# Seven block products of 256 x 512 x 512 in place of eight for most of the second feed-forward products, with weight sums made by accumulating transfers

## The reference

```python
x = x + jnp.concatenate([ya, yb, yc], axis=-1) @ w_out
u = _rms(x, norm2) @ w_ff1                  # 1024 -> 4096
return x + jnp.square(jax.nn.relu(u)) @ w_ff2   # 4096 -> 1024
```

## Time and profile before

| | |
|---|---|
| median of 3 runs | 2929.8 us (2923.84 to 2934.4) |
| profiled execution, span from the first to the last instruction | 2923.6 us |
| mean granted clock of TensorE | 0.969 of 2.4 GHz |
| PE / DVE / ACT / POOL busy | 95% / 49% / 34% / 6% |
| bytes moved by DMA | 216.83 MB, 74 GB/s over the span |

### The profile page before, as it was taken

How to read it: one execution, slowest core, us unless ns; L and a number is a source line. 1 busy time by engine, 2 the same in 40 slices (tenths; PEclk the granted TensorE clock), 3 DMA queues, 4 the chain that set the end, 5 groups by cost and what they waited for, 6 DMA issues and landing times.

```text
span 2923.6 us, 45193 instructions
## 1 busy us (share of the span) xinstructions
PE 2783.6 (95%) x20028; PEld 2299.7 (79%) x20028; DVE 1440.3 (49%) x2242; ACT 988.4 (34%) x1490; POOL 170.2 (6%) x166
## 2 busy tenths in 40 slices
PE   8989999999989999999999799999999897999998
PEld 7877888878768888887768778888887587788887
DVE  4575533344475444433454574343634645743436
ACT  4344322233344232323342233232333522332422
POOL 0200000001100000000013300000000033000000
PEclk9998999999989999999989899999999898999999
DMA  5102222223003222221000033222220001132221
GB/s 192 50 1 97 87 101 96 92 73 114 17 8 136 94 94 101 93 92 52 15 1 30 20 128 115 90 102 90 85 73 29 1 3 46 73 130 101 87 101 58
DMA packets 31011, 216.83 MB, mean 74 GB/s; under 512 B 3680, under 2 KB 3936, under 8 KB 6368
## 3 DMA queue, kind: packets, MB, share of 16 engines
q1 hardware_dynamic: 30816, 213.94, 20.2%
HBM read 211.83 MB, written 2.10 MB: 73 GB/s over the span
## 4 chain that ended last, share of the span: by engine, by line
PE 88%; DVE 8%; ACT 2%; issue 1%; PEld 0%; PEldq 0%; DMA 0%; ACTq 0%; SPq 0%; DVEq 0%
PE PS L570 81%; PE PS L573 3%; PE PS L771 2%; DVE SC L1381 2%; DVE X L1389 1%; DVE R L1381 1%; DVE SM L1392 1%; PE PS L1185 1%; PE PS L1135 1%; DVE LN L1381 0%; PE PS L855 0%; DVE SM L1381 0%; ACT LN L2172 0%; PE PS L764 0%; PEld PS L570 0%
## 5 line engine op out<-in xcount | busy, mean ns | idle before, releaser
L570 PE MATMUL PS<-H,SPL 128*128 128x512 f32 (+1 forms) x4560 | 1054.2, 391 | 5.5 <-DVE H L1389 4.0
L570 PEld LDWEIGHTS PS<-H,SPL 128*128 128x128 f32 (+1 forms) x4560 | 851.5, 188 | 188.5 <-issue 7.0
L1381 DVE TENSOR_TENSOR SPL<-RAW,SPL 128x2048 fp32r<-128x2048 f32 (+3 forms) x192 | 429.6, 2239 | 680.5 <-ACT SPL L2172 677.5
L2172 ACT ACTIVATE SPL<-RAW 128x2048 fp32r<-128x2048 f32 (+3 forms) x192 | 358.0, 1868 | 783.0 <-PE PS L570 754.8
L570 PE MATMUL PS<-SPL,Uu 128*128 128x512 f32 x2592 | 589.8, 389 | 0.0
L570 PEld LDWEIGHTS PS<-SPL,Uu 128*128 128x128 f32 x2592 | 486.5, 188 | 101.0
L570 PE MATMUL PS<-SPL,H 128*128 128x512 f32 (+2 forms) x2016 | 432.1, 375 | 2.3 <-DVE SPL L1381 1.6
L570 PEld LDWEIGHTS PS<-SPL,H 128*128 128x128 f32 x2016 | 363.7, 189 | 69.2 <-DVE SPL L1381 2.1
L2172 ACT ACTIVATE R<-PS 128x512 f32<-128x512 f32 (+1 forms) x154 | 88.5, 584 | 187.0 <-PE PS L570 156.3
L1381 DVE TENSOR_TENSOR R<-R,PS 128x512 f32<-128x512 f32 (+1 forms) x98 | 64.8, 661 | 106.6 <-PE PS L570 91.2
L2172 ACT ACTIVATE Uu<-R 128x512 fp32r<-128x512 f32 x108 | 68.3, 632 | 142.2 <-DVE R L1381 142.2
(11 more groups left out here) (240 smaller groups left out, 2481.7 us busy)
## 6 DMA issues: line engine op xcount, KB each, us to landing
RAW<-in_wA SPq DMA_DIRECT2D x84, 1024.0 KB, 4.8
RAW<-in_wB SPq DMA_DIRECT2D x84, 1024.0 KB, 4.8
RAW<-in_wAo SPq DMA_DIRECT2D x8, 1024.0 KB, 4.8
RAW<-in_wBo SPq DMA_DIRECT2D x8, 1024.0 KB, 5.0
LN<-in_ln SPq DMA_DIRECT2D x4, 1024.0 KB, 6.6
P<-in_pB SPq DMA_DIRECT2D x2, 1920.0 KB, 9.1
RAW<-in_wBm SPq DMA_DIRECT2D x4, 704.0 KB, 4.0
X<-in_x SPq DMA_DIRECT2D x4, 512.0 KB, 5.6
```

The lines of the kernel that those rows point to most:

```text
L570: return pe.matmul(out, l_, r_, start=start, stop=stop)
L1381: return v.tensor_tensor(out, a, b, o)
L2172: return a.activation(out, in_, f, scale=scale)
```

## The change

In a changed pass (all four in layers 0 and 1, the first two in each layer of the second half) the second product is computed as a 2 x 2 block product with seven multiplications. The left operand A has tokens 0 to 255 (EARLY) or 256 to 511 (LATE) by features 0 to 511 or 512 to 1023 of the pass; the right operand B has the same halves of features by the two halves of the output columns, so a block of B is one weight group. Each of the seven products (P1, P2, P5, P3, P6, P7, P4, in this order) is 24 matmuls in two banks. P3 is accumulated on P5's banks after P5 was added to X, P6 on P1's, P7 on P6's. DVE makes the four sums of A (S1 to S4, in place). The four sums of B (T1 to T4) are made by transfers that POOL issues with an add: T3 = B12 + B22 and T1 = B11 + B12 and T2 = T1 + B22 from device memory onto a loaded group, T4 = B21 + T2 from one on-chip buffer onto another. T1 is issued when B11 has been split, T2 when T1 has, T4 when T2 has landed and B21 has been split. The raw groups have four buffers (the two of `RAW`, `RW2`, and `LN`, which held norm tables); each of the seven factors is split into high and low as a group was, so a pass has seven splits in place of four for the second product. DVE makes 16 additions into X per pass, in place of 8.

In layers 0 and 1 the norm's factor now goes in ahead of the square: PE spreads the four tiles' roots over a bank (`spread_roots`, between the first two groups of the stretch), ACT copies it to `RB`, DVE computes max(u, 0) x RB out of the bank (`squared`), and ACT squares in place. A's high and low parts are made 1024 columns at a time (`high_operand`, `low_operand`). The program's scratch for descriptors that POOL writes is 1024 bytes per partition, in place of the default.

```diff
+N_UP = ((4, 4, 4, 4), (4, 4, 4, 4), (8, 8, 6), (8, 8, 6))
+PRODUCTS = ("P1", "P2", "P5", "P3", "P6", "P7", "P4")
+FACTORS = ("B11", "B21", "T1", "B22", "T2", "T3", "T4")
+HELD = {"B11": "B11", "B21": "B21", "T1": "B11", "B22": "B22", "T2": "B11", "T3": "B12", "T4": "B21"}
+SUMS = {"T3": 1, "T1": 1, "T2": 2, "T4": 3}
+CHAINED = 3
+BLOCKS = {"B11": 0, "B21": 1, "B12": 2, "B22": 3}
...
+            if p in QUADS[l]:
+                held = dict(zip(("B11", "B21", "B22", "B12"), ring))
+                landed = {name: load(l, at + BLOCKS[name], slot)[1] for name, slot in held.items()}
+                summed = {name: (name != "T3", 16 * ((1 if name == "T3" else CHAINED) * len(quads) + k)) for name, k in SUMS.items()}
+                quads.append((l, p, len(splits), at, held, landed, summed))
+                for name in FACTORS:
+                    split(held[HELD[name]], landed.get(name), summed.get(name))
+                last[held["B11"]] = len(splits)
+                ring = [held[n] for n in ("B22", "B12", "B21", "B11")]
...
+        A11, A21, A12, A22 = (RU[k][:, :, ts_] for k in range(2) for ts_ in (EARLY, LATE))
+        S3, S2, S1, S4 = A11, A11, A21, A12
+        RB = SM[:, 0:512]
...
+        LEFT = {"P1": ("A11", 1), "P2": ("A12", 3), "P5": ("S1", 4), "P3": ("S4", 6), "P6": ("S2", 5), "P7": ("S3", 2),
+                "P4": ("A22", 7)}
+        PBANKS = {"P1": (0, 1), "P2": (2, 3), "P5": (4, 5), "P3": (4, 5), "P6": (0, 1), "P7": (0, 1), "P4": (6, 7)}
...
+            def spread_roots(l):
+
+                pe.wait_ge(s.nr, 8 * (l + 1))
+                bank_free(4)
+                for t in range(4):
+                    ins = mm(bank(4)[:, t * 128:(t + 1) * 128], rms[t][:, 1:2].to_broadcast([128, 128]), C("ident"))
+                ins.then_inc(s.gtr, 1)
+                free[4] = (s.rc, l + 1)
+
+            def quad(key):
+
+                base, ready = n["xadd"], n.get("ul", 0)
+                added_to = {("P6", 0): 1, ("P6", 1): 2, ("P3", 0): 5, ("P3", 1): 6, ("P7", 0): 9, ("P7", 1): 10}
+                for name in PRODUCTS:
+                    i = at["group"]
+                    at["group"] += 1
+                    wh_, wl_ = slot(i)
+                    which, lows = LEFT[name]
+                    ah, al = operand(OPERANDS[which][0])
+                    pe.wait_ge(s.lo, i + 1)
+                    pe.wait_ge(s.ul, ready + lows)
+                    goes_on = (name, 0) in added_to
+                    for b in range(2):
+                        if goes_on:
+                            pe.wait_ge(s.xadd, base + added_to[name, b])
+                        else:
+                            bank_free(PBANKS[name][b])
+                        out = bank(PBANKS[name][b])
+                        for k in range(4):
+                            sl = slice(k * 256 + b * 128, k * 256 + b * 128 + 128)
+                            wh, wl = wh_[:, k * 512:(k + 1) * 512], wl_[:, k * 512:(k + 1) * 512]
+                            pe.matmul(out, ah[:, sl], wh, start=k == 0 and not goes_on, stop=False,
+                                      skip_group_check=True)
+                            pe.matmul(out, ah[:, sl], wl, start=False, stop=False, skip_group_check=True)
+                            ins = pe.matmul(out, al[:, sl], wh, start=False, stop=k == 3, skip_group_check=True)
+                        assert done_mm(ins) == full_at[(*key, name), b]
+                    assert at["mm"] == used_at[i]
+                for b, e in enumerate((12, 14, 3, 4, 7, 8, 15, 16)):
+                    free[b] = s.xadd, base + e
+                n("xadd", 16)
...
+            def low_operand(which, ks=slice(0, 4)):
+
+                i, a_ = OPERANDS[which]
+                hi, lo = operand(i)
+                v.wait_ge(s.uh, n("uh"))
+                ins = tt(four(lo)[:, ks], a_[:, ks], four(hi)[:, ks].bitcast(f32), ALU.subtract)
+                if ks.stop == 4:
+                    ins.then_inc(s.ul, 1)
+                    n("ul")
+
+            def row_sum(which):
+
+                if which == "S3":
+                    ins = tt(S3, A11, A21, ALU.subtract)
+                elif which == "S1":
+                    ins = tt(S1, A21, A22, ALU.subtract)
+                elif which == "S2":
+                    ins = stt(S2, A22, -1.0, S3, ALU.mult, ALU.subtract)
+                else:
+                    ins = tt(S4, A12, S2, ALU.add)
+                ins.then_inc(s.us, 1)
+                v.wait_ge(s.us, n("us"))
...
+                def add(name, b, t, h, first=False, op=ALU.add):
+                    ps = bank(PBANKS[name][b])
+                    v.wait_ge(s.mm, full_at[(*key, name), b])
+                    if (h, t) in last_sum:
+                        v.wait_ge(s.xadd, last_sum[h, t])
+                    if first and beta is not None:
+                        stt(Xh(h, t), Xh(h, t), beta, ps, ALU.mult, op).then_inc(s.xadd, 1)
+                    else:
+                        tt(Xh(h, t), Xh(h, t), ps, op).then_inc(s.xadd, 1)
+                    last_sum[h, t] = n("xadd")
...
+                low_operand("A12", slice(2, 4))
+                row_sum("S1")
+                low_parts()
+                low_operand("S1")
+                add("P1", 0, 0, 0, True)
+                add("P1", 1, 1, 0, True)
+
+                row_sum("S2")
+                add("P2", 0, 0, 0)
+                low_operand("S2")
+                row_sum("S4")
+                low_parts()
+                add("P2", 1, 1, 0)
+
+                low_operand("S4")
+                add("P5", 0, 2, 1, True)
+                low_parts()
+                add("P5", 1, 3, 1, True)
+
+                add("P3", 0, 0, 1, True)
+                low_parts()
+                add("P3", 1, 1, 1, True)
+
+                low_operand("A22")
+                low_parts()
+                add("P6", 0, 0, 1, op=ALU.subtract)
+                ended(0)
+                add("P6", 1, 1, 1, op=ALU.subtract)
+                ended(1)
+
+                low_parts()
+                add("P7", 0, 2, 0, True)
+                add("P7", 0, 2, 1, op=ALU.subtract)
+                add("P7", 1, 3, 0, True)
+                add("P7", 1, 3, 1, op=ALU.subtract)
+
+                low_parts()
+                add("P4", 0, 2, 0)
...
+                    def squared(q, b):
+                        v.wait_ge(s.mm, full_at[(l, "up", p, q), b])
+                        stt(RU[q][:, b], bank(sets[q][b]), 0.0, RB, ALU.max, ALU.mult).then_inc(s.fv, 1)
+
+                    paid()
+                    low_parts()
+                    low_parts()
+                    v.wait_ge(s.rc, l + 1)
+                    for b in range(4):
+                        squared(0, b)
...
+            def quad(l, p):
+
+                j, at, held, landed, summed = quads[l, p]
+
+                def block(name):
+                    return stream[first_load(l) + at + BLOCKS[name]][0]
+
+                B11, B21, B12 = (raw_slots[held[name]][:, 0:2048] for name in ("B11", "B21", "B12"))
+
+                g.wait_ge(s.raw[held["B12"]], landed["B12"])
+                g.dma_start(B12, block("B22"), accum_op=ALU.add).then_inc(s.tx, 16)
+                g.wait_ge(s.lo, j + 1)
+                g.dma_start(B11, block("B12"), accum_op=ALU.add).then_inc(s.ty, 16)
+                g.wait_ge(s.lo, j + 3)
+                g.dma_start(B11, block("B22"), accum_op=ALU.add).then_inc(s.ty, 16)
+                g.wait_ge(s.lo, j + 2)
+                g.wait_ge(s.ty, summed["T2"][1])
+                g.dma_start(B21, B11, accum_op=ALU.add).then_inc(s.ty, 16)
+
```

More of the change, by code:

```diff
@@ new lines, with first_load, groups_of, first_group @@
+SUMS = {"T3": 1, "T1": 1, "T2": 2, "T4": 3}
+CHAINED = 3
+BLOCKS = {"B11": 0, "B21": 1, "B12": 2, "B22": 3}
+def first_load(l):
+    return l * LOADS_A if l < 2 else 2 * LOADS_A + (l - 2) * LOADS_B
+def groups_of(l):
+    return INPUTS[l] + 4 + sum(N_UP[l]) + sum(7 if p in QUADS[l] else N_DOWN for p in range(len(N_UP[l])))
+def first_group(l):
+    return sum(groups_of(k) for k in range(l))
+def load_plan():
+    loads, splits = [], []
+    used = [0] * 4
+    last = [None] * 4
+    def lands(slot):
+        used[slot] += 1
+        return 16 * used[slot]
+    def load(l, what, slot):
+        loads.append((l, what, slot, last[slot]))
+        last[slot] = None
+        return slot, lands(slot)
+    def split(slot, landed, summed=None):
+        splits.append((slot, landed, summed))
+        last[slot] = len(splits)
+    def plain(l, what, slot):
+        split(*load(l, what, slot))
+    turn = 0
+    quads = []
+    for l in range(4):
+        for k in range(INPUTS[l] + 4):
+            plain(l, k, turn % 2)
+            turn += 1
+        at = INPUTS[l] + 4
+        ring = [0, 1, 2, 3] if turn % 2 == 0 else [1, 0, 2, 3]
+        for p, n_up in enumerate(N_UP[l]):
+            if QUADS[l] and p not in QUADS[l]:
+                ring = [x for x in ring if x != 3]
+            elif not QUADS[l]:
```

(42 more changed lines are left out.)

299 lines of the change are left out of this document (231 added, 68 removed).

## The result

| | before | changed |
|---|---|---|
| median of the executions timed with the result | 2924.5 us (20) | 2937.4 us (20) |
| ratio, 95% interval | 1 | 1.0043 (1.0028 to 1.0057) |
| the same two kernels once more, later (17 and 12 executions) | 2927.3 us | 2927.7 us, 1.0004 (0.9985 to 1.0023) |
| profiled execution, span | 2923.6 us | 2925.4 us |

The forecast was 2895 us. The change takes 288 matmuls away and the kernel is 0 to 0.4% slower for it: some 40 us were won on PE and were lost again inside the same stretches.

The account below looks back on a forecast made before the run. TensorE (PE), busy 95% of the span, was taken as the bound. 65.3 us of matmuls less 1.7, 13.6 and 4.0 gave 46.0; less 11.0 for transfers, 35 off 2929.8: 2895 us, range 2868 to 2952.

Parts of the forecast that it names:

- 288 matmuls x 0.2269 = 65.3 us off: PE, twelve changed passes: seven block products need 168 matmuls where 192 stood, saving 65.3 us.
- roots +1.7: PE, first two layers: four small matmuls each to spread the norm's roots add 1.7 us, without a wait.
- P3's new wait: PE waits at P3 for DVE's addition of P5: 1.7 us eight times, 1.0 four times, 13.6 and 4.0 us.
- T1 and T3 at nothing: These adding transfers are issued over 14 us before their splits, covered by the up product, so cost nothing.
- T2 at 8.5: T2's adding transfer in each changed pass takes 8.5 us to landing, chosen between 7.7 and 9.1.
- T4 at 8.5 + half of 2.9: T4's landing takes 8.5 us plus 1.45 for the next pass's load; P7 is delayed, 11 us over twelve passes.
- the pair: T2's and T4's landings together per changed pass: 17.6 us available, 18.5 expected, 0.9 over.
- The clock: Feed-forward stretches: longer stops could lower the granted clock from 1.00; unsized, attached only to the slow rival.
- The prediction without T4: Total saving before charging the chained adding transfers: 65.3 - 1.7 - 13.6 - 4.0 = 46.0 us.
- in between: Rival: landings of 9.1 us and the full 2.9, 3.5 over per pass, 42 us lost, 2926 us; chance 0.11.
- the slow rival: Rival: T2 and T4 landing at 11.2 us delay T4's split, 75 us lost, 2959 us; chance 0.19.
- The estimate of 6.8 us: Side estimate for one adding transfer, 2.0 + 2 x 2.4; T2 and T4 stay under 17.6, saving 46 us.

Follow-up runs that it names:

- e2: The changed kernel with P6's two additions on DVE moved ahead of T4's low part; 0.9878 of before, once more 0.9871.
- e5: The changed kernel with DVE's additions of P1, P2 and P5 reordered so P5's banks are added sooner; 0.9944 of before.
- e6: e5's order of additions plus e2's edit, on the changed kernel; 0.9790 of before, 2870.8 us.
- e8: e6 with the last low part of each changed pass moved behind P4's two additions on DVE; 0.9804 of before.
- e1: The changed kernel with the next pass's load held on SP's queue until T4 has landed; 0.9873 of before, 2890.1 us.
- e7: e6 plus e1's holding of the next pass's load; 0.9787 of before, 2865.0 us.
- e3: The changed kernel with T4's transfer adding block B22 from device memory instead of the on-chip sum (T4 then wrong); 1.0004 of before.
- e4: The changed kernel with no accumulating transfers, T1 to T4 split from the plain blocks (sums missing); 0.9880 of before, 2892.5 us.
- c1: The changed kernel itself run again, unaltered, for a second profile; 1.0004 of before.

## Why the prediction was wrong, point by point

- **288 matmuls x 0.2269 = 65.3 us off, and roots +1.7: right.** Inside e2 a pass repeats after 83.6 us. Before it was 384 x 0.2269 = 87.1; less 24 matmuls (5.45) and plus 1.7 for P3 it should be 83.4.
- **P3's new wait, 1.7 us x 8 and 1.0 x 4: right.** Measured 1.70 x 8 and 1.23 x 4, 18.5 us for the 17.6 forecast. e5 and e6 show that it is DVE's order that makes it.
- **T1 and T3 at nothing, T2 at 8.5: right.** They land in 8.0 us; T4's issue stands 8.67 behind T2's.
- **T4 at 8.5 + half of 2.9: the step that failed.** It said that the next pass's load "takes up to 2.9 us of the same 16 engines; I charge half". Alone the transfer takes 7.0 (the guess was on the safe side), but two loads fall on it, not one, the first in full and the second by half or less: 12.3, which is 5.3 for what was charged with 1.45 (T4 of the first pass 12.5). T1's low part ended 6.4 us into that pass, as walked, the pair took 21.5 and not 18.5, and P7 was late by 29.8 us in eleven passes where the sum had 11 in twelve. The place was right: P7 waits for P6's addition, behind T4's low part.
- **The clock: left out of the sum.** The text had it as a rider to one rival only ("longer stops could also let the granted clock fall"). It took 13.6 us. Besides, each stop of P7 costs some 0.4 us beyond its shown idle time, about 4 in all: the idle time is counted from the modelled end of the last matmul, 0.39 us after its start where the next would have started after 0.23, and the first matmul behind the stop delays the next one.
- **Not foreseen:** the end of layer 0, 3.1 us (the two waits that e8 takes away).

By the stretches of the profiles (the last one to the end of the span): from before to e2, 9.7, 12.9, 8.2 and 9.4 us are off, 40.2 together. The prediction without T4 had 46.0; 0.9 (P3), 3.1 (layer 0's end) and about 2.4 (0.2 us per pass) make up the difference. From e2 to the changed kernel 14.2, 15.8, 10.7 and 7.7 come back, 48.4 us: waits 29.8, half clock 13.6, the 4, and 1 for five half-clock matmuls at the start of the fourth stretch that e2 has not. That leaves the four stretches 8.2 us longer than before. The span shows 1.8 longer, since this execution reached the first of them at 290.4 and not at 297.0, in code that the change does not touch.

Of the rivals, *in between* had the right size: 21.1 us for the pair and 42 us given back, 2926; it had a chance of 0.11. Its reason was another one, transfers of 9.1 us with one load beside the second, and it had no term for the clock, so that its time comes near the measured one is luck. The second load is let go when T3's low part is done, 24.1 us into the first pass, and the order of instructions ahead of the result had that place, 0.8 us ahead of the landing that was forecast (6.4 + 18.5 = 24.9). With both charged in full, 8.5 for T2 and 8.5 + 2 x 2.9 = 14.3 for T4 make 22.8, more than the 21.4 from which the slow rival decides, so that charge would have turned the sign of the forecast, though 14.3 is 2 us more than T4 took.

A rule beside this: the Trainium skill (Collectives: The Full Stack, the section on the bandwidth ceiling) says that an adding transfer reads two sources through one ring, at half the rate. The trace agrees: in the window 356.6 to 363.6 of e1, where T4 runs alone, the DMA share is 0.75, that is 5.2 us of all 16 engines for 1024 KB, against 2.9 for a plain load, 1.8 times. The estimate of 6.8 us, made ahead of the result from this page and the Trainium skill's DMA: Bandwidth & Descriptors (the anatomy of one DMA), is for a transfer by itself, and such ones take 7.0 to 8.0 here by their medians; it has no term for the loads beside it, which decided.

## What to carry to other kernels

Where an engine with an in-order queue waits for a transfer, look at what stands behind that wait and is already complete: moving two additions of 0.7 us ahead of one wait was worth as much here (0.988) as taking away the contention (0.987) or all the transfers (0.988), and with the second such edit the change gave 2.1%. When a transfer joins a dependent chain, count every other transfer that the same program issues within its landing; charging each in full gave an upper bound here (12.8 for 10.4 to 12.5 us). A stop of PE costs more than its length where the granted clock falls after it (here 1.5 to 3.0 us more).

## What the runs showed of the hardware

- An accumulating transfer of 1024 KB from device memory lands in 8.0 us (median; 7.8 to 9.3), one from buffer to buffer in 6.9 to 7.6 in ten passes of e1 and in 9.1 in another (6.9 to 8.6 in e7, which holds the loads too); with two plain loads of 1024 KB issued beside it, 10.4 to 12.5 from a buffer (changed kernel), and 10.0 to 12.2 from device memory (e3). I had expected the buffer as the source to be the dearer one.
- With a plain load issued within 0.6 us of it, the transfer's first packet came 3.6 to 5.3 us after its issue in ten of the eleven passes of the changed kernel that have one, and after 1.45 in the other; with none beside it, 1.4 to 1.5 us after (e1).
- Stops of PE of 1.2 to 1.7 us were followed by no half-clock matmul in e1, e2 and e4 (twelve stops each). After stops of 2.0 to 3.8 us the granted clock fell to 0.50 for 5 to 13 matmuls in eight cases of nine in the changed kernel, and in seven of ten in e5; after 3.10 us in the one and after 2.01, 3.27 and 3.09 in the other it did not. The two other profiles with such stops have it in eight of ten (c1) and five of eight (e3). The length of the stop alone does not decide it: the clock fell after 2.06 us in c1 and stayed at 1.00 after 3.27 in e5.
